# Softmax scaling on VectorE behind its reciprocal, in a two-block float32 transformer kernel

## The reference

```
s = q @ k.T * 64 ** -0.5 + table
p = exp(s - max(s)) / sum(exp(s - max(s)))      # softmax over the keys
o = p @ v
```

## Time and profile before

| | before |
|---|---|
| median of 3 runs | 3275.93 us (3275.39 to 3276.64) |
| the profiled execution's own time | 3276.04 us |
| its span, first to last instruction | 3274.2 us |
| TensorE matmul busy | 3012.9 us, 92% |
| VectorE busy | 1467.6 us, 45% |
| ScalarE busy | 799.2 us, 24% |
| GpSimd busy | 1008.8 us, 31% |
| mean granted TensorE clock | 0.960 |

### The profile page before, as it was taken

The page is one execution under the profiler, slowest core; times in us unless marked ns, Lnnn a source line. Parts: engine busy times, 40 slices in busy tenths (PEclk is TensorE's granted clock), DMA queues, the critical chain, the costliest instruction groups (busy, mean ns, idle before and its releaser), DMA issues.

```text
span 3274.2 us, 40376 instructions
## 1 busy us (share of the span) xinstructions
PE 3012.9 (92%) x14394; PEld 2408.0 (74%) x14394; DVE 1467.6 (45%) x1877; ACT 799.2 (24%) x1156; POOL 1008.8 (31%) x395
## 2 busy tenths in 40 slices
PE   5888776999999599999999999999999999899997
PEld 4565455877887488887777888888888777688886
DVE  7455555112111642473227642474246332664247
ACT  3333331011001321213332222222122233222121
POOL 2221121000000244443333444444444333344442
PEclk8899887999999799999999999999999999999998
DMA  3111111654565232232222332323233222233232
GB/s 119 47 41 55 37 41 71 206 200 176 187 211 178 74 101 90 93 109 73 82 77 78 96 104 88 106 81 98 94 96 106 77 86 73 77 93 105 86 99 79
DMA packets 87046, 326.66 MB, mean 100 GB/s; under 512 B 9664, under 2 KB 10816, under 8 KB 86592
## 3 DMA queue, kind: packets, MB, share of 16 engines
q1 hardware_dynamic: 86976, 325.71, 30.2%
HBM read 323.58 MB, written 2.10 MB: 99 GB/s over the span
## 4 chain that ended last, share of the span: by engine, by line
issue 62%; PE 18%; POOL 15%; DVE 2%; DMA 1%; ACT 1%; POOLq 1%; DVEq 0%; SPq 0%
POOL WL L422 15%; PE TURN L646 3%; PE SCORE L646 3%; PE GEMM L646 2%; PE GEMM L673 1%; PE SCORE L632 1%; PE DEN L660 1%; DMA E_PANEL<-experts 1%; PE GEMM L483 1%; PE OUT L660 1%; PE GEMM L485 1%; PE GEMM L484 1%; PE TURN L632 1%; PE GEMM L623 0%; POOLq L163 0%
## 5 line engine op out<-in xcount | busy, mean ns | idle before, releaser
L422 POOL TENSOR_TENSOR WL<-RAW,WH 128x1024 fp32r<-128x1024 f32 (+1 forms) x379 | 993.1, 2621 | 1644.6 <-ACT WH L898 1644.6
L483 PE MATMUL GEMM<-XH,WH 128*128 128x512 f32 x2152 | 857.3, 398 | 37.2 <-POOL WL L422 32.0
L484 PE MATMUL GEMM<-XL,WH 128*128 128x512 f32 x2152 | 844.0, 392 | 0.0
L485 PE MATMUL GEMM<-XH,WL 128*128 128x512 f32 x2152 | 843.8, 392 | 0.0
L898 ACT CAST WH<-RAW 128x1024 fp32r<-128x1024 f32 (+1 forms) x379 | 417.9, 1104 | 1374.5 <-PE GEMM L485 1358.0
L483 PEld LDWEIGHTS GEMM<-XH,WH 128*128 128x128 f32 x2152 | 408.6, 190 | 132.9 <-issue 37.4
L485 PEld LDWEIGHTS GEMM<-XH,WL 128*128 128x128 f32 x2152 | 408.0, 190 | 86.8
L484 PEld LDWEIGHTS GEMM<-XL,WH 128*128 128x128 f32 x2152 | 408.7, 190 | 85.6 <-issue 2.5
L483 PE MATMUL GEMM<-AH,WH 128*128 128x512 f32 (+1 forms) x1072 | 424.6, 396 | 50.8 <-DVE AL L1245 18.0
L484 PE MATMUL GEMM<-AL,WH 128*128 128x512 f32 (+1 forms) x1072 | 420.3, 392 | 0.0
L485 PE MATMUL GEMM<-AH,WL 128*128 128x512 f32 (+1 forms) x1072 | 419.8, 392 | 0.0
(11 more groups left out here) (312 smaller groups left out, 2818.1 us busy)
## 6 DMA issues: line engine op xcount, KB each, us to landing
RAW<-up SPq DMA_DIRECT2D x176, 512.0 KB, 3.5
E_PANEL<-experts SPq DMA_DIRECT2D x128, 512.0 KB, 4.5
RAW<-mix SPq DMA_DIRECT2D x96, 512.0 KB, 3.5
RAW<-down SPq DMA_DIRECT2D x64, 704.0 KB, 4.0
RAW<-experts SPq DMA_DIRECT2D x64, 512.0 KB, 4.4
RAW<-panels SPq DMA_DIRECT2D x43, 512.0 KB, 3.6
AR<-bias SPq DMA_DIRECT2D x16, 320.0 KB, 3.8
X<-xT SPq DMA_DIRECT2D x1, 2048.0 KB, 11.1
```

What stands on the lines that cost most here:

```text
L422: pool.tensor_tensor(WL[slot][:, 0:width], RAW[slot][:, 0:width], f32(WH[slot][:, 0:width]), ALU.subtract).then_inc(split_lo, c.add(split_lo))
L483: pe.matmul(ps, whb, hi, start=(begin and j == 0), stop=False)
L484: pe.matmul(ps, whb, lo, start=False, stop=False)
L485: mm = pe.matmul(ps, wlb, hi, start=False, stop=(end and j == len(blocks) - 1))
```

## The change

The second half of the softmax moves from ScalarE to VectorE. ScalarE's `norms` and its calls go away, with the semaphore `recips_ready`; VectorE's `recips` becomes `norms`, which waits on its own reciprocal (`chain`, L1177) and then issues one `tensor_scalar` for each head. TensorE's `turns` waits on the same semaphore `probs_ready` as before, which VectorE now raises. The values computed are the same.

```diff
-            def norms(tiles, i):            # ScalarE
-
-                act.wait_ge(recips_ready, c.next(recips_ready))
-                for h in range(2):
-                    p = probs(tiles, i, h)
-                    act.activation(p, p, ACT.Copy, scale=stat(2, i, h)).then_inc(probs_ready, c.add(probs_ready))
...
                     if i:
                         turned_probs(tiles, i - 1)
-                    if i < QT:
-                        norms(tiles, i)
...
-            def recips(i):                  # VectorE
+            def norms(tiles, i):
 
                 v.wait_ge(exp_done, c.next(exp_done, 2))
-                v.reciprocal(stat(2, i, 0, 2), stat(1, i, 0, 2)).then_inc(recips_ready, c.add(recips_ready))
+                chain(v.reciprocal(stat(2, i, 0, 2), stat(1, i, 0, 2)))
+                for h in range(2):
+                    p = probs(tiles, i, h)
+                    v.tensor_scalar(p, p, stat(2, i, h), None, ALU.mult).then_inc(probs_ready, c.add(probs_ready))
...
                     logits(tiles, i, bias)
-                    recips(i)
+                    norms(tiles, i)
```

More of the change, by code:

```diff
@@ L103 @@
     "out_full out_taken den_full den_taken operand_ready sumsq_ready squares_ready normed high_ready moved std_ready vec_in "
-    "dve_step exp_done recips_ready probs_ready turn_ready qk_ready conv_done conv_ready "
+    "dve_step exp_done probs_ready turn_ready qk_ready conv_done conv_ready "
     "sin_ready sin_done gate_ready gate_done rows_ready m_args_ready m_exp_ready "
@@ L298, in build @@
          sumsq_ready, squares_ready, normed, high_ready, moved, std_ready, vec_in, dve_step,
-         exp_done, recips_ready, probs_ready, turn_ready, qk_ready, conv_done, conv_ready, sin_ready,
+         exp_done, probs_ready, turn_ready, qk_ready, conv_done, conv_ready, sin_ready,
          sin_done, gate_ready, gate_done, rows_ready, m_args_ready, m_exp_ready, act_out, route_args,
@@ L1128, in _ @@
                     exps(NEAR, 0)
-                    norms(NEAR, 0)
                     round_hi()
@@ L1132, in _ @@
                     turned_probs(NEAR, 0)
-                    norms(NEAR, 1)
                     c.skip(scores_taken, 2)
@@ L1137, in _ @@
                     turned_probs(NEAR, 1)
-                    norms(NEAR, 2)
                     exps(NEAR, 3)
-                    norms(NEAR, 3)
                     round_hi()
@@ L1660, in _ @@
                     logits(NEAR, 0, bias_of)
-                    recips(0)
+                    norms(NEAR, 0)
                     v.wait_ge(turned_full, c.next(turned_full, 2))
@@ L1672, in _ @@
                         v.tensor_copy(AB[:, b * T:(b + 1) * T], ps[:, :]).then_inc(scores_taken, c.add(scores_taken))
-                    recips(1)
+                    norms(NEAR, 1)
                     take(tile(GATE_A, i * 2))
@@ L1676, in _ @@
                     logits(NEAR, 2, bias_of)
-                    recips(2)
+                    norms(NEAR, 2)
                     den = den_in()[:, :].rearrange("p (two c r) -> p two c r", two=2, r=NA_ROWS)
@@ L1685, in _ @@
                     logits(NEAR, 3, bias_of)
-                    recips(3)
+                    norms(NEAR, 3)
                     take(tile(GATE_B, i * 2))
```

## The result

| | before | changed |
|---|---|---|
| median of 19 runs each, side by side | 3275.39 us (3267.15 to 3279.14) | 3281.57 us (3275.16 to 3288.14) |
| ratio to before, 95% interval | | 1.0021, 1.0013 to 1.0029 |
| the profiled execution's own time | 3276.04 us | 3283.71 us |
| its span | 3274.2 us | 3281.5 us |
| mean granted TensorE clock in it | 0.960 | 0.958 |

The change made the kernel slower by 0.21%, 6.9 us on 3275.39 (4.3 to 9.5); the two medians lie 6.2 us apart. The forecast was 3278.0 us and "within 0.2%". The three runs of before that were known then lay within 1.3 us of each other; its 19 runs lie within 12.

What follows compares the result with a forecast made beforehand. TensorE, its matmuls busy 92% of the span, was taken as the bound. 3276.04 + 2.4 (causal) - 0.3 (cross) = 3278.1 us, as a median 3278.0 us, 0.06% slower; range 3274.3 to 3282.0 us.

Steps and rivals of the forecast that it cites:

- Price of one scaling: One VectorE scaling takes 0.28 us at 128 columns, 0.35 at 256, 0.41 at 384 and 0.48 at 512.
- Causal attention, the chain: Units 1 to 3 of a mixer: next logits queue behind VectorE's scalings, exponentials wait, the attention ends 0.6 us later.
- 4 x 0.6 = +2.4 us: Causal attention's total: 0.6 us later in each of four mixers; bounds +0.8 and +4.0 us.
- The clock falls in the causal attention: Rival: longer TensorE waits drop its clock in units 2 and 3; +6.4 us a mixer, 3302 us; chance 3%.
- The test for it: Sign that the prediction is wrong: units 1 to 3 of the causal attention show a clock below 1.00.
- Cross attention, -0.15 a pair: Two pairs: unit 0's transposes start 0.16 us earlier and this stays; -0.3 us for both, bounds -0.5 and +0.2.
- Neighbourhood attention, 0: 32 units: no effect, since unit 2's transposes start 8.8 us behind the reciprocal; without that cover 10 us.
- The port, 0 counted: Neighbourhood scalings wait for GpSimd at the shared port, some as long as 1 to 2.5 us, inside the cover; 0 us.
- its relief: Rival: ScalarE's freed time leaves the causal chain in units 1 to 3, 13.7 us gained, median 3262; chance 4%.
- The port's wait: Rival: neighbourhood scalings held up by GpSimd subtractions delay TensorE, 8 x 1.9 = 15 us, 3291 us; chance 5%.
- No measurable shift: Rival: the late causal exponentials are absorbed by unseen slack, 3276 us; chance 10%.
- The base: Starting time for the range: median 3275.93 us of the kernel before, with a run spread of 0.6 us below.

Runs made afterwards that it cites:

- c4: Kernel before, ScalarE still scaling, plus two spare VectorE scalings behind each reciprocal of the causal and cross attention; 3278.05 us, ratio 1.0013.
- c2: Kernel before with the scaling moved to VectorE in the causal and cross attention only; 3277.29 us, ratio 1.0015.
- c1: The kernel before, unchanged, run and profiled a second time; 3273.90 us, ratio 1.0006.
- c3: Kernel before with the scaling moved to VectorE in the neighbourhood attention only; 3277.48 us, ratio 1.0009.
- d2: Changed kernel with spare matmuls in TensorE's waits in the causal attention, before the values of units 2 and 3; 3276.83 us, ratio 1.0004 to before.
- d4: Kernel before with head 0 scaled by VectorE and head 1 by ScalarE in the causal and cross attention; 3272.86 us, ratio 0.9996.
- d3: Changed kernel with a second, spare pair of VectorE scalings in the causal units; 3290.72 us, ratio 1.0049 to before.
- e2: Changed kernel with spare matmuls in TensorE's waits in the mixers outside the attention; 3278.13 us, ratio 1.0010 to before.
- e1: Kernel before with spare matmuls in TensorE's waits in the mixers outside the attention; 3264.91 us, ratio 0.9975.
- d1: Kernel before with spare matmuls in TensorE's waits in the causal attention, before the values of units 2 and 3; 3275.89 us, ratio 1.0000.
- e4: Kernel before with the shared pair of d4 and the spare matmuls of both e1 and d1; 3268.36 us, ratio 0.9976.

## Why the prediction was wrong, step by step

- **What bounds the kernel, and where the move acts**: right. The neighbourhood attention shows no change, the causal attention does.
- **Price of one scaling**: right. 280, 353 and 487 ns were measured at 128, 256 and 512 columns, for 0.28, 0.35 and 0.48.
- **Causal attention, the chain**: right in mechanism and size. The attention is 0.57 us longer where the clock holds (11.77 to 12.34), for 0.6; c4 shows that VectorE's order alone makes it. The exponential of unit 2 starts 2.92 us behind the first logits (121.14 to 124.06) for 2.61 before (0.31 late, forecast 0.36), the one of unit 3 0.55 late (5.85 for 5.30, forecast 0.6), the values of unit 2 0.56 late (129.30 from 121.14, before 127.96 from 120.36).
- **"4 x 0.6 = +2.4 us"**: this is the step that failed. It let the chain's own lengthening be all that the causal attention pays, and put the clock at nothing in the sum. In the profiled execution two attentions of four were 13.35 and 13.27 us long with the clock down. The first three kernels with the delay (changed, c2, c4) have stages of 331.4, 328.4 and 328.5 us, the three with before's causal code (before, c1, c3) 321.8, 323.1 and 322.2: 7.1 us on average, of which 4 x 0.57 = 2.3 is the chain and 4.8 the clock. The timing of the changed kernel against before gave 6.9.
- **Where these 4.8 us lie**: in part in the attentions. In mixer 3 the clock fell in all three kernels; from its unit 1 to the cross attention they take 102.7 to 102.8 us for 99.8 to 100.6, 1.9 us more than the chain's 0.57. In mixer 0 it fell in one, for 2.7 us, in mixers 1 and 2 in none. That is (3 x 1.9 + 2.7) / 3 = 2.8. The other 2.0 are longer low stretches outside the attentions: behind that of mixer 2 all three spend 10.2 us at the lower clock, before, c1 and c3 3.4 to 6.8. d2 has that stretch too. What makes them longer wasn't tried.
- **The rival "The clock falls in the causal attention"** was the right mechanism, with a chance of 3%. Its condition, "from the first idle stretch that is long enough, and the longest grows only by 0.6 us", was used as an argument against it; it is the point at which it decides. Its price was too high for the place (6.4 us a mixer, in four): in mixer 0 the clock falls 10.3 us into the attention, during unit 3, so 1.0 us is lost there and 1.7 in the product, and it falls in some mixers only.
- **The test for it** held: "wrong if the window of units 1 to 3 has a clock below 1.00", and it has 0.89 in mixer 0.
- **Cross attention, -0.15 a pair**: right where it arises, not in the sum. The transposes of unit 0 start 0.44 behind the reciprocal's end for 0.59, in the second pair 0.45 for 0.60. But to its last value the first pair takes 13.87 us for 13.94, and both together 33.98 for 33.90, with their low stretches in different places: the -0.3 is not seen, and is too small for the timing.
- **Neighbourhood attention, 0**: right by the trace (41.89 us a pair in every kernel), not settled by the timing (c3).
- **The port, 0 counted**: right in the sum, and the wait of unit 2 for the end of the subtraction was worked out rightly. But "1 to 2.5 us where GpSimd runs" was wrong: the longest of 112 scalings took 487 ns. The reason is where they start: 16 of them meet only the last 0.28 to 0.36 us of a subtraction, the others none, where the long instructions of the earlier trace rows start near its beginning. The Trainium skill, SBUF — State Buffer, section SBUF: two separate sides, has the port pair that a VectorE op in a 2-port mode shares with GpSimd locked for an instruction's whole length. The trace agrees: each of the 16 ends only behind the subtraction that it meets.
- **The other rivals** fell: in c4 ScalarE keeps its scalings, and the attention is as long as in the changed kernel, so its relief is worth nothing behind VectorE's full pair. (In d4 half the relief and half the delay cancel.) The port's wait reaches no row of TensorE. "No measurable shift", at 10%, is excluded by the interval.
- **The base**: the median of three runs, 3275.93, was good, but their spread of 1.3 us was taken for the kernel's. 19 runs spread over 12 us, and that the range of 3274.3 to 3282.0 holds the time is luck: without the 1.2 us that it kept for the clock, in the products ahead of the tight units, it would have ended at 3280.8. Nor is 0.2% the limit of a measurement: with 19 runs of each kernel the interval is 0.08% to either side.

What is shown and what isn't: the causal delay is shown by c4, d3 and the timelines. That the clock makes the difference between a loss that can't be measured and this one rests on d2 against the changed kernel (1.0004 against 1.0021, intervals that overlap by a hair) and on e2 against e1 (13 us with 2.3 us of chain). The runs without a profile say the same: their mean granted clock averages 0.9588 in the changed kernel, 0.9595 in c2 and 0.9593 in c4, but 0.9615 over the 97 runs of before beside the experiments, 0.9618 in d1 and 0.9616 in d2. At 2.2 to 2.5 us for 0.001 the changed kernel's 0.0027 is 6 to 7 us, an estimate from these rows.

How many attentions fall in an execution that wasn't profiled isn't known. Over all profiles the attention of 12.34 us without filling inside it lost the clock in 8 of 16 cases: in mixer 3 in 4 of 4, in mixer 0 in 2 of 4, in mixers 1 and 2 in 1 of 4 each. The one of 11.77 or 11.75 lost it in none of 32 (8 of them filled, in d1 and e4), the filled one of d2 in none of 4, the one of d3 in 4 of 4.

## What to carry to other kernels

An edit that makes TensorE wait a little longer in a stretch where it already idles a quarter of the time is not priced by its own length: look whether the granted clock in that stretch is still whole, and give the case that it falls a real chance and the price of the product behind it. Before a scaling is moved to the engine where it is shorter, see what is queued behind it there: a 0.63 us pair ahead of the next unit's first step cost more than a 0.9 us pair on the engine that waits for that step anyway. And take a kernel's spread from more than three runs when a fifth of a per cent is the question.

## What the runs showed of the hardware

- The granted clock can hang on 0.57 us: an attention of 11.77 us kept it whole in 32 of 32 cases, one of 12.34 us in 8 of 16. Windows of the same instructions have 1.00 or 0.82 to 0.89, and 16 matmuls take 1.09 or 1.97 us. The Trainium skill, TensorE: Matmul & The Clock Gate, section HAM oscillation — how this bites in real kernels, says that idle gaps bring the clock down and shows a kernel that loses by it. The trace agrees (with the waits filled, in d2, no attention fell), and adds that the same program in one execution falls in one mixer and not in the next, and that in mixer 0 no wait of TensorE in the attention was over 1.95 us.
- Filling one set of waits may make another fall: with the gaps of e2 filled the attention fell in 4 of 4, without that filling in 4 of 12 (changed, c2, c4). One profile doesn't make that a rule, and why wasn't tried; it stays open.
- A VectorE scaling that starts beside a GpSimd subtraction ends behind it, and how long it is depends on how much of the subtraction was left: 0.28 to 0.36 us here, and at most 475 ns for 192 columns, but 3516 ns for an instruction of the earlier trace rows that started with it.
- Spare matmuls in waits pay where they keep the clock whole in front of large products (e1, 0.25% faster, 24 us less at the lower clock), and pay nothing where it was whole before (d1).
- Over the 19 runs of the changed kernel, the one with a mean granted clock of 0.956 took 3288 us and the two with 0.961 about 3275.5: some 2.5 us for each 0.001.
